# Router steps inside half products, a top-two selection from eight maxima, and an earlier masking of own heads

## The reference

```python
    y_d = o_d.reshape(b, t, W_DIFF) @ w_o_diff
    y_s = o_s.reshape(b, t, W_DSA) @ w_o_dsa
    merged = jax.nn.sigmoid(gt_d) * y_d + jax.nn.sigmoid(gt_s) * y_s
    return x + merged @ w_out, rows

def hier_moe(x, g_ffn, w_group, w_router, w_gate, w_up, w_down):
    h = rmsnorm(x, g_ffn).reshape(b * t, d)
    g_logits = jnp.dot(h, w_group).astype(jnp.float32)
    g_prob = jax.nn.softmax(g_logits, axis=-1)
    g_sel = jnp.argmax(g_logits, axis=-1)
    g_w = jnp.take_along_axis(g_prob, g_sel[:, None], axis=-1)
    e_logits = jnp.dot(h, w_router).astype(jnp.float32).reshape(-1, N_GROUPS, EXPERTS_PER_GROUP)
    e_in_group = jnp.take_along_axis(e_logits, g_sel[:, None, None], axis=1)[:, 0]
    top_val, top_idx = lax.top_k(e_in_group, TOP_K_EXPERTS)
    top_w = jax.nn.softmax(top_val, axis=-1) * g_w
    ...
    def add_expert(acc, params):
        wg, wu, wd, c = params
        act = jax.nn.silu(h @ wg) * (h @ wu)
        return acc + (act @ wd) * c[:, None], None
```

## Time and profile before

| | |
|---|---|
| three runs | 1294.77, 1293.09, 1288.33 us (median 1293.09) |
| profiled execution | 1290.44 us |
| its span, first to last instruction | 1288.6 us |
| mean granted clock of TensorE | 0.956 |
| busy in the span: PE, DVE, ACT, POOL | 1104.0, 500.4, 235.1, 184.8 us |
| read from HBM | 290.03 MB |

### The profile page before, as it was taken

The page is one execution under the profiler, slowest core; times in us unless marked ns, Lnnn a source line. Parts: engine busy times, 40 slices in busy tenths (PEclk is TensorE's granted clock), DMA queues, the critical chain, the costliest instruction groups (busy, mean ns, idle before and its releaser), DMA issues. The chain is left out here.

```text
span 1288.6 us, 16258 instructions
## 1 busy us (share of the span) xinstructions
PE 1104.0 (86%) x6061; PEld 569.8 (44%) x6061; DVE 500.4 (39%) x1291; ACT 235.1 (18%) x506; POOL 184.8 (14%) x178
## 2 busy tenths in 40 slices
PE   4989999879899999989889968999777777777873
PEld 3544444434445454633235645555444444444441
DVE  3326885995586667532123552311111111111110
ACT  2102221110233233340102421111111110101010
POOL 1012201220000000000200001323222222212211
PEclk9999999888999899989899978999999999999997
DMA  5141022106364533459828467999999999999991
GB/s 177 31 145 57 35 99 74 57 34 214 106 197 125 161 104 102 131 195 338 305 90 339 165 224 277 396 404 388 399 408 402 400 403 400 403 412 400 404 391 49
DMA packets 77126, 304.15 MB, mean 236 GB/s; under 512 B 22406, under 2 KB 22406, under 8 KB 64758
## 3 DMA queue, kind: packets, MB, share of 16 engines
q1 hardware_dynamic: 61622, 273.47, 55.7%
q0 software_dynamic: 9824, 16.98, 4.7%
q10 hardware_dynamic: 5600, 12.65, 2.6%
HBM read 290.03 MB, written 29.66 MB: 248 GB/s over the span
## 5 line engine op out<-in xcount | busy, mean ns | idle before, releaser
L368 PE MATMUL p_z<-k_w,k_xT 128*128 128x512 f32 (+2 forms) x528 | 215.9, 566 | 3.8 <-DMA k_w<-in_w_in 3.3
L368 PEld LDWEIGHTS p_z<-k_w,k_xT 128*128 128x128 f32 (+1 forms) x528 | 95.5, 195 | 112.4 <-issue 108.7
L776 PE MATMUL a_G<-k_w,k_xT 128*128 128x512 f32 x256 | 134.5, 649 | 2.5 <-ACT k_x L834 2.5
L1915 DVE TENSOR_TENSOR e_den<-e_sig,e_G 128x256 f32<-128x256 f32 x32 | 13.5, 421 | 276.7 <-ACT e_sig L1820 276.7
L1825 ACT ACTIVATE e_y<-e_Y,x_share 64x512 f32<-64x512 f32 x64 | 43.7, 683 | 313.6 <-PE e_Y L1728 296.1
L1946 POOL DMA_INDIRECT out_y_p<-e_y,x_table x32 | 45.0, 1408 | 196.6 <-ACT e_y L1825 154.1
L776 PEld LDWEIGHTS a_G<-k_w,k_xT 128*128 128x128 f32 x256 | 45.4, 198 | 62.8 <-issue 57.6
L1920 DVE TENSOR_TENSOR e_a<-e_den,e_U 128x256 f32<-128x256 f32 x32 | 13.5, 421 | 126.0 <-PE e_U L1716 126.0
L1120 PE MATMUL g_ring<-k_w,k_oT 128*128 128x512 f32 x128 | 59.8, 613 | 0.0
L848 ACT ACTIVATE a_prob<-a_masked,a_nb 128x128 f32<-128x128 f32 (+3 forms) x64 | 36.0, 562 | 127.1 <-DVE a_nb L941 127.1
L134 POOL DMA_INDIRECT k_rows<-token_rows,x_table x32 | 31.2, 976 | 190.7 <-PE e_TX L1710 164.0
(11 more groups left out here) (341 smaller groups left out, 1500.6 us busy)
## 6 DMA issues: line engine op xcount, KB each, us to landing
k_w<-in_w_in SPq DMA_DIRECT2D x11, 2048.0 KB, 7.9
k_w<-in_w_gate SPq DMA_DIRECT2D x11, 2048.0 KB, 45.2
k_w<-in_w_up SPq DMA_DIRECT2D x11, 2048.0 KB, 44.9
k_xT<-in_w_down SPq DMA_DIRECT2D x11, 2048.0 KB, 45.5
k_oT<-in_w_gate SPq DMA_DIRECT2D x11, 2048.0 KB, 44.4
k_side<-in_w_up SPq DMA_DIRECT2D x11, 2048.0 KB, 45.1
x_page<-in_w_down SPq DMA_DIRECT2D x11, 2048.0 KB, 45.0
x_merged<-in_w_gate SPq DMA_DIRECT2D x10, 2048.0 KB, 43.5
```

The source lines that it names most:

```text
L368: last = nc.tensor.matmul(z[u % 3][0:p, 0:WIDTH[k]], s.xT[:, j, 128 * i:128 * i + p], s.w[:, c % 2, j, 0:WIDTH[k]], start=j == 0, stop=j = ...
L776: last = nc.tensor.matmul(G[u % 2][:], s.xT[:, j, 128 * i:128 * i + 128], s.w[:, q % 2, j, :], start=j == 0, stop=j == KD - 1)
L1915: v.tensor_tensor(den[:], sig[:], G[j][:, 0:HW], ALU.mult).then_inc(chain, 1)
```

## The change

It does the following:

1. `own_heads(2)` is done before the merge of product 13, `samples_out(1, ...)` before that of product 15 (VectorE), and `extract(2)` follows product 14 (TensorE). Before, all three stood behind the slots.
2. `summing` takes a list of steps that it issues after its fourth matmul. `logit(NT)`, `logit(2)`, and the steps `norm(3, 0)`, `tables(NT)`, `rank(2)` move into half products.
3. `decide` finds the two best experts by one operation of eight maxima and by replacing matched values, and not by two rounds of maximum, comparison, index and minimum.
4. `place` does both choices at once and writes only the first half of the one-hot rows; `share` writes the other.
5. On VectorE `decide(NT)` goes ahead of `add_x(2, 1)`, and `add_x(3, 0)` and `add_x(3, 1)` behind `decide(2)` and `share(2)`. On ACT `copy_norm(2, 1)` goes ahead of `square(2)`.

```diff
-            def summing(i, h):
+            def summing(i, h, between=()):
...
                     for j in range(KD):
                         last = nc.tensor.matmul(S[h][:], x[:, j, :], w_out[:, h, j, :], start=j == 0, stop=j == KD - 1)
+                        if j == 3:
+                            for step in between:
+                                step()
...
+                if sl == SLOTS_A - 2:
+                    extract(2)
...
             turn(1)
-            extract(2)
             pe.wait_ge(oT_ready, 3)
...
             rank(1)
-            summing(2, 1)
-            logit(NT)
+            summing(2, 1, [lambda: logit(NT)])
             norm(2, 0)
             turn(3)
+            norm(2, 1)
+            rank(NT)
             tables(1)
-            summing(3, 0)
-            rank(NT)
-            norm(2, 1)
-            logit(2)
-            tables(NT)
-            summing(3, 1)
-            norm(3, 0)
-            rank(2)
+            summing(3, 0, [lambda: logit(2)])
+            summing(3, 1, [lambda: norm(3, 0), lambda: tables(NT), lambda: rank(2)])
+            tables(2)
             norm(3, 1)
             logit(3)
-            tables(2)
             rank(3)
             tables(3)
...
             copy(3)
+            copy_norm(2, 1)
             square(2)
             scale(2)
             shares(NT)
-            copy_norm(2, 1)
...
+                link(v.memset(both, -TAKEN))
+                link(v.memset(one, -TAKEN))
                 dve.wait_ge(wr_in, 64)
...
-                link(v.tensor_reduce(on(ev0), on(Lm), AX.X, ALU.max))
-                link(v.tensor_scalar(on(eeq), on(Lm), on(ev0), -99.0, ALU.is_equal, ALU.mult))
-                link(v.tensor_tensor(on(ecand), on(eeq), iota(NE)[0:p], ALU.add))
-                link(v.tensor_reduce(on(low), on(ecand), AX.X, ALU.min))
-                link(v.tensor_scalar(oh[:, 0, :], on(ecand), on(low), None, ALU.is_equal))
-                link(v.scalar_tensor_tensor(on(Lm2), oh[:, 0, :], MASKED, on(Lm), ALU.mult, ALU.add))
-                link(v.tensor_reduce(on(ev1), on(Lm2), AX.X, ALU.max))
-                v.tensor_tensor(on(dd), on(ev1), on(ev0), ALU.subtract).then_inc(differ, 1)
...
-                v.tensor_tensor(on(C), oh[:, 0, :], oh[:, 1, :], ALU.add).then_inc(decided, 1)
+                link(v.max(on(top), on(Lm)))
+                v.tensor_tensor(on(dd), top[0:p, 1:2], top[0:p, 0:1], ALU.subtract).then_inc(differ, 1)
+                link(v.tensor_copy(both[0:p, 0:2], top[0:p, 0:2]))
+                link(v.match_replace(on(Lm2), on(both), on(Lm), TAKEN))
+                v.tensor_scalar(on(C), on(Lm2), TAKEN, None, ALU.is_equal).then_inc(decided, 1)
+                dve.wait_ge(decided, a + 1)
+                link(v.tensor_copy(one[0:p, 0:1], top[0:p, 0:1]))
+                link(v.match_replace(on(Lm2), on(one), on(Lm), TAKEN))
+                link(v.tensor_scalar(oh[:, 0, :], on(Lm2), TAKEN, None, ALU.is_equal))
+                link(v.tensor_tensor(oh[:, 1, :], on(C), oh[:, 0, :], ALU.subtract))
...
-                for k in range(2):
-                    link(v.tensor_tensor(prank[0:p], RK, oh[:, k, :], ALU.mult))
-                    link(v.tensor_reduce(rank[:, k:k + 1], prank[0:p], AX.X, ALU.add))
-                    v.tensor_scalar(Rk[0:p, k], bcast(iota(CAP)[0:p], 2, 1), rank[:, k:k + 1], None, ALU.is_equal)
+                link(v.tensor_tensor(prank[0:p], bcast(RK, 2, 1), oh, ALU.mult))
+                link(v.tensor_reduce(rank, prank[0:p], AX.X, ALU.add))
+                v.tensor_tensor(Rk[0:p, :, 0, :], bcast(iota(CAP)[0:p], 2, 1), bcast(rank, CAP, 2), ALU.is_equal)
...
+                v.tensor_tensor(Rk[0:p, :, 1, :], bcast(iota(CAP)[0:p], 2, 1), bcast(rank, CAP, 2), ALU.is_equal)
                 dve.wait_ge(weighed, 2 * a + 2)
...
+                if sl == SLOTS_A - 3:
+                    own_heads(2)
+                if sl == SLOTS_A - 1:
+                    samples_out(1, O[:, 0:16])
                 merge_tile(sl)
...
             share(1)
+            decide(NT)
             add_x(2, 1)
-            decide(NT)
-            add_x(3, 0)
             place(NT)
             share(NT)
             decide(2)
-            add_x(3, 1)
+            add_x(3, 0)
             place(2)
             share(2)
+            add_x(3, 1)
             decide(3)
```

More of the change, by code:

```diff
@@ L1025, in merge @@
         geq, gcand, pen, dgr, gexp = (small[:, 4 * n:4 * n + NG] for n in range(5))
-        gm, gmin, ev0, ev1, low, dd, dl, gs, gden = (small[:, 24 + n:25 + n] for n in range(9))
-        Lm, Lm2, eeq, ecand, pen1, C = (small[:, 40 + 32 * n:72 + 32 * n] for n in range(6))
+        gm, gmin, dd, dl, gs, gden = (small[:, 24 + n:25 + n] for n in range(6))
+        Lm, Lm2, C = (small[:, 40 + 32 * n:72 + 32 * n] for n in range(3))
         unfilled, early = small[0:CAP, 232:232 + NE], small[0:CAP, 264:264 + NE]
-        prank = small[:, 296:296 + NE]
+        prank = small[:, 296:296 + 2 * NE].rearrange("p (k e) -> p k e", k=2)
+        top, both, one = (small[:, 368 + 8 * n:376 + 8 * n] for n in range(3))
         Rk = branch[:, 0:4 * CAP].rearrange("p (k h c) -> p k h c", k=2, h=2)
@@ L1575, in share @@
                 a, p = order(i), ROWS[i]
-                oh, wt = s.oh[0:p, i], s.wt[0:p, i]
+                oh, rank, wt = s.oh[0:p, i], s.rank[0:p, i], s.wt[0:p, i]
+                v.tensor_tensor(Rk[0:p, :, 1, :], bcast(iota(CAP)[0:p], 2, 1), bcast(rank, CAP, 2), ALU.is_equal)
                 dve.wait_ge(weighed, 2 * a + 2)
@@ L1628, in _ @@
                     weights_turned(SOFTMAX_AT[sl - 1])
-            own_heads(2)
-            samples_out(1, O[:, 0:16])
             branches()
```

4 lines of the change are left out of this document (removed).

## The result

| | before | after |
|---|---|---|
| median of 14 runs each | 1291.61 us (1283.65 to 1295.90) | 1281.64 us (1277.69 to 1286.68) |
| profiled execution, its span | 1290.44, 1288.6 us | 1285.33, 1283.5 us |
| mean granted clock of TensorE | 0.956 | 0.960 |
| busy PE, DVE | 1104.0, 500.4 us | 1099.8, 494.5 us |

The ratio of the means is 0.9934, 95% interval [0.9916, 0.9951]: 8.5 us faster, and the median 10 us lower. The forecast was 1287.0 and its range began at 1283.5, so the time fell out of the range on the fast side. The mechanisms of the prediction are nearly all in the trace. The path to the load of expert 3 became 6.2 us shorter in the shown pair of executions where 4.7 were forecast, and three further executions of the kernel before have a path that is 3 us longer than the shown one. The second point took experiments.

A forecast was written before the change was run, and what follows sets the result against it. The experts' weight stream was taken as the bound, its start set by the path to expert 3's load; 2.98 + 0.66 + 1.1 = 4.7 us off the 1291.7 us mean gave 1287.0 us, range 1283.5 to 1292.5.

The forecast's parts named there:

- The bound: Experts' weight stream from HBM: from expert 3's load it takes 480.4 us regardless; each microsecond saved before counts fully.
- The head: Last values' masking and extraction among the products: 1.56 us less waiting plus 1.42 us less low clock, 2.98 us.
- Rival (2): Low clock at the samples' small products stays although the wait goes: gain 3.3 us, 1288.4 us, chance 0.13.
- The middle: Small products inside half products: waits of 0.39 and 1.27 us go, two steps add 1.0 us; gain 0.66 us.
- Rival (4): TensorE's waits in mid-product eat the gain there and part of the earlier saving: 1290 us, chance 0.10.
- The tail: Behind the last half product: table path 2.4 us shorter, but the rows' landing lets only 1.1 us count.
- Rivals (1): Row store lands last already or later, so the faster table gains nothing: gain 3.6 us, 1288.1 us, chance 0.15.
- (3): Rows land before the table even so, so its whole 2.4 us counts: gain 6.0 us, 1285.7 us, chance 0.12.
- (5): Full clock returns only behind expert 0's gate and up products: 5.6 us more, 1292.6 us, chance 0.05.

The follow-up runs named there:

- the middle alone: Kernel before with only the small products moved inside half products and the matching VectorE and ACT orders, old decide and place: ratio 0.9969.
- the run without the head: Changed kernel with masking, extraction and copy of the last values behind the slots again: ratio 0.996, median 1286.57 us.
- The head alone: Kernel before with only masking, extraction and copy of the last values moved among the products: ratio 0.9993.
- the selection alone: Kernel before with only the eight maxima and matched values in decide and both choices at once in place: ratio 0.9988.

## Why the prediction was wrong

**The bound** was right. The stream from the load of expert 3 is a constant (479.8 to 481.7 us in fourteen traces), and the microseconds of the path count one for one.

**The head** was right in kind and small in size: 3.51 us, not 2.98. The wait gave 1.84 and not 1.56, because the extraction costs TensorE some 0.8 us between products where I had charged the 1.05 of its row; the clock gave 5.28 - 3.61 = 1.67 and not 1.42. Rival (2), that the low clock stays, did not happen. The low clock went with the wait in all four traces of before, but not in that of the middle alone.

**The middle** was too small. By the shown pair it gave 76.48 - 74.82 = 1.66 us at the last addition and not 0.66. Of this 0.63 is the stop in the router product of tile 1, which no other execution of before has; the new order accounts for 1.03. The two steps moved into the half product cost 0.53 + 0.47 = 1.00, as I had set them. The 0.4 us that I had not counted are small steps that overlap better: tile 2's router product takes 1.71 us inside the half product where it took 1.90, and the steps in a row ahead of the half product (3, 0) save some 0.25. But this term holds for the shown execution only. The other three take 79.10 us for the same stretch and not 76.48, because of the 3.25 us at the lower clock: over all traces the middle is worth 78.44 - 74.82 = 3.6 us. The 1.6 us of slack of add_x(3, 0) held: it ends at 743.28, and TensorE wants it at 744.88. Rival (4), waits in mid-product, is refuted by the trace after and by the middle alone.

**The tail** was right where it counts. I had given the table 2.4 us and the gather 1.1, because the rows would bind. The gather gained 14.33 - 13.03 = 1.30 in the shown pair, and 2.25 with the second trace of the changed kernel. The table gained 13.21 - 9.50 = 3.71 us from the end of the last half product on: 1.96 in the selection (4.45 to 2.49, with the maxima at 0.20 and the replacement at 0.17, near what I took), 0.52 in placing, and 1.23 that I had missed. The two steps moved ahead of that end no longer stand behind it, so `decide(3)` starts 3.52 us behind it and not 4.75. It changed nothing, since the rows bound. The rows' landing went as I had it. In the trace after the DMA engines' share is 0.04 in the quarter microsecond before 761.75 and 0.00 behind it (length, POOL busy and count, clock, DMA share, GB/s); POOL starts at 763.00, and of these 1.25 us some 0.94 are what POOL took after the table's release as well (768.72 to 769.66).

```profile
761.50:761.75 0.25, 0.00 (x0) 0.50 0.04 16
761.75:762.00 0.25, 0.00 (x0) 0.50 0.00 0
```

The Trainium skill (DMA: Bandwidth & Descriptors, "Anatomy of one DMA") puts most of some 2 us down to the receipt for the last byte, above all towards HBM, for transfers that GpSimd issues. The rows' store is issued by ScalarE; its trace leaves 0.3 us behind the last packets, so the 2 us that the prediction carried over to it don't hold here.

Rivals (1) and (3) are thus wrong, and (5), the clock in front of expert 0, too: the gate product takes 5.63 and 5.76 us in the two traces of the changed kernel. It took 5.27 in the shown execution of before, but 5.8 in the other three. In the variants it takes 5.1 to 6.1 us, and 6.5 with the selection alone; the loss of 5.6 us came nowhere.

**The step that failed is the middle term of the sum**, 0.66 us, and with it the 4.7: I read its size off one execution of before and set it against the mean of the times. The shown pair gives 6.15 us on the path, 1.5 more than forecast. The other three executions of before are 3.0 us longer than the shown one, by a stretch at the lower clock in the last half products for which the sum has no term. None of the six traced executions with both the new head and the new middle has it. Over all traces the path is 125.5 us before (mean of four) and 116.6 after (mean of two), 8.9 us: 3.5 in the head, 3.6 in the middle, 1.8 in the tail, nothing behind the gather. The pooled times agree within their error: means of 1290.7 before (61 runs) and 1283.0 after (26 runs), 7.7 us, by about 1.6 either way (95%).

Not all of the miss is this term. The median of 1281.64 lies 5.4 us below the forecast. About 3.0 of it is the gain, 7.7 and not 4.7. About 1.0 is the mean of before that I started from, 1291.7 from four executions. The other 1.4 is the draw of these 14 runs: all 26 have a mean of 1283.0, half a microsecond outside the range.

A clue was there: the shown execution, at 1290.44 us, was 2.7 below the median of the runs. I took the clock as something that the kernel's order fixes; the same kernel got it both ways.

**What stays open.** That the stretch at 745 us comes from the stops before it is argued, not shown. It is there in 3 of 6 traces whose middle has the 1.27 us or a 0.79 us wait, and in none of the 8 without it; but the run without the head had one elsewhere. The three are executions of the kernel before, on two chips. The head alone and the selection alone, which have the old middle too and show no stretch, ran on a third chip. So a difference between chips is not excluded, nor is chance with so few traces. The timed gains of the parts alone (0.1%, 0.3% and 0.1%, each with some 0.25% either way) add up to 0.5%, the whole gave 0.5 to 0.7%: the times can't tell whether the parts depend on each other.

## What to carry to other kernels

Profile the kernel before more than once before pricing a change of TensorE's order: here a second one showed that 3 us of the path came and went. When a faster step sits beside a transfer that ends at about the same moment, count only the slack between the two, and look at what shares the DMA engines with that transfer; here the table released the gather again only once a 2 MB load had been moved away from the rows' store. The merge part ended sooner with one gather in it than with two, so a gather that the next part needs late was better issued there.

## What the runs showed of the hardware

- On 32 columns and 128 partitions the eight maxima take 0.20 us and the match with replacement 0.17, plus 0.09 for the value load; at 256 columns they took 0.43 and 0.41. The step in width of eight costs only a factor of two.
- The same instruction stream, behind the same wait of 1.27 us, was granted 1.00 in one execution and 0.50 for 6.8 us in three others; the stretch cost 3.25 us.
- A 2 MB weight load beside a gather of 64 rows more than doubled the gather's landing, 3.0 to 7.5 us; beside the rows' store it held the store up by at least 1.5 to 2.4 us.
- The experts' part starts 5.0 us behind the first of two gathers, 8.9 with a load beside them, and 3.6 behind a single one.
